# VectorE's order of work in the MLP chunks of a two-layer decoder trunk: two modulation rows instead of three ahead of an up block, and low parts and evacuations of the down half reordered

## The reference, cut to what matters

```python
u = modulate(h, sh_f, sc_f)                                  # u = h * (1 + sc_f) + sh_f
y = jnp.square(jax.nn.relu(u @ mlp_w_up[layer])) @ mlp_w_down[layer]
h = layer_norm(DEEPNORM_ALPHA * h + (1 + g_f) * y, ...)      # up: 1024 -> 4096, down: 4096 -> 1024
mod = (silu(c) @ ada_w[layer] + ada_b[layer])                # six vectors of 1024; two more for K/V
```

## Time and profile before

| | |
|---|---|
| time, median of 3 runs | 2198.84 us (2197.66 to 2198.94) |
| profiled execution | 2198.61 us, span of its trace 2196.9 us |
| TensorE | 2144.9 us busy, 98% of the span, 9984 matmuls |
| VectorE | 1419.3 us, 65% |
| ScalarE | 820.0 us, 37% |
| GpSimd | 373.6 us, 17% |
| granted TensorE clock | 0.997 of full speed on average |

### The profile page before, as it was taken

How to read it: one execution, slowest core, us unless ns; L and a number is a source line. 1 busy time by engine, 2 the same in 40 slices (tenths; PEclk the granted TensorE clock), 3 DMA queues, 4 the chain that set the end, 5 groups by cost and what they waited for, 6 DMA issues and landing times.

```text
span 2196.9 us, 28310 instructions
## 1 busy us (share of the span) xinstructions
PE 2144.9 (98%) x9984; PEld 1730.2 (79%) x9984; DVE 1419.3 (65%) x2223; ACT 820.0 (37%) x1457; POOL 373.6 (17%) x273
## 2 busy tenths in 40 slices
PE   6999999999999999999999999999999999999998
PEld 5888888878887787788887876677888888888886
DVE  7423656578576676776768566767747547557556
ACT  4201445161224234233347456546222422422432
POOL 0000220010033032130200022321003303303304
PEclk9999999999999999999999999999999999999999
DMA  7434653314413423314122110211211021021021
GB/s 291 142 98 133 117 131 101 105 39 134 130 63 95 125 66 115 113 59 134 48 96 85 43 39 20 78 58 33 64 58 58 21 74 57 20 75 57 19 77 77
DMA packets 52433, 183.96 MB, mean 84 GB/s; under 512 B 7472, under 2 KB 7648, under 8 KB 52352
## 3 DMA queue, kind: packets, MB, share of 16 engines
q1 hardware_dynamic: 44640, 161.50, 22.8%
q0 software_dynamic: 4944, 16.96, 3.6%
q10 hardware_dynamic: 2768, 4.41, 0.5%
HBM read 174.43 MB, written 8.42 MB: 83 GB/s over the span
## 4 chain that ended last, share of the span: by engine, by line
issue 44%; PE 41%; POOL 8%; DVE 3%; ACT 2%; DMA 1%; SPq 1%; POOLq 0%; ACTq 0%; DVEq 0%
PE ps L2054 11%; PE ps L2056 11%; PE ps L2055 11%; POOL whi L678 4%; POOL wlo L678 2%; PE ps L2519 1%; POOL h_blocks L673 1%; PE ps L2549 1%; PE ps L2533 1%; DMA resid<-in_xt 1%; PE ps L2157 1%; PE ps L2298 1%; PE ps L2283 1%; PE ps L2287 1%; DVE stats L1572 0%
## 5 line engine op out<-in xcount | busy, mean ns | idle before, releaser
L2054 PE MATMUL ps<-uhi,whi 128*128 128x512 f32 x1152 | 451.6, 392 | 11.3 <-DVE wlo L1700 5.0
L2055 PE MATMUL ps<-ulo,whi 128*128 128x512 f32 x1152 | 448.4, 389 | 0.0
L2056 PE MATMUL ps<-uhi,wlo 128*128 128x512 f32 x1152 | 448.3, 389 | 0.0
L2054 PE MATMUL ps<-whi,uhi 128*128 128x512 f32 x704 | 288.2, 409 | 2.4 <-ACT resid L1111 2.2
L2056 PE MATMUL ps<-whi,ulo 128*128 128x512 f32 x704 | 276.1, 392 | 0.0
L2055 PE MATMUL ps<-wlo,uhi 128*128 128x512 f32 x704 | 275.4, 391 | 0.0
L2054 PEld LDWEIGHTS ps<-uhi,whi 128*128 128x128 f32 x1152 | 216.2, 188 | 65.2 <-issue 7.3
L1740 DVE TENSOR_TENSOR resid<-ps,resid 128x512 f32<-128x512 f32 x336 | 217.9, 680 | 54.8 <-PE ps L2056 53.7
L2056 PEld LDWEIGHTS ps<-uhi,wlo 128*128 128x128 f32 x1152 | 216.3, 188 | 45.3
L2055 PEld LDWEIGHTS ps<-ulo,whi 128*128 128x128 f32 x1152 | 216.3, 188 | 44.0
L1021 ACT ACTIVATE h_blocks<-ps 128x512 f32<-128x512 f32 x96 | 57.2, 596 | 516.5 <-PE ps L2056 516.5
(11 more groups left out here) (300 smaller groups left out, 3542.1 us busy)
## 6 DMA issues: line engine op xcount, KB each, us to landing
stage<-in_stream SPq DMA_DIRECT2D x276, 512.0 KB, 3.6
aux<-in_early SPq DMA_DIRECT2D x8, 512.0 KB, 7.1
early_place<-in_early SPq DMA_DIRECT2D x8, 512.0 KB, 14.2
resid<-in_xt SPq DMA_DIRECT2D x8, 512.0 KB, 15.9
resid<-in_x POOLq DMA_DIRECT2D x8, 512.0 KB, 9.5
resid_dram<-resid ACTq DMA_DIRECT2D x8, 512.0 KB, 2.6
resid<-resid_dram POOLq DMA_DIRECT2D x8, 512.0 KB, 3.6
out<-resid SPq DMA_DIRECT2D x7, 512.0 KB, 2.6
```

The costliest lines, as they stand in the source:

```text
L2054: pe.matmul(dst, left_hi, right_hi, start=start, stop=False, skip_group_check=more)
L2055: pe.matmul(dst, left_hi, right_lo, start=False, stop=False, skip_group_check=more)
L2056: return pe.matmul(dst, left_lo, right_hi, start=False, stop=stop, skip_group_check=more)
```

## The change

In the seven-product chunks of layer 0 the load stream and VectorE take two modulation rows ahead of `up_low(2)` and not three; one stays between `up_low(2)` and `up_low(3)`, and five and not four follow later. In the down half of all twelve chunks VectorE's order changes in three places: `low_of(4, 1, 6)` goes ahead of the evacuation of P4,0; the evacuations of P1,2 and P1,3 go ahead of `up_low(8)`; and `up_low(9)` goes behind `add("P6", 0)` and `low_of(4, 8, 14)`. No instruction is added or taken away.

```diff
     for c in range(CHUNKS):
         if c in SEVEN:
             w(*[W_MLP0 + 8 * c + j for j in SEVEN_LOADS[:4]])
-            ada(SC_KV + c, range(3))
+            ada(SC_KV + c, range(2))
             w(W_MLP0 + 8 * c + 2)
-            ada(SC_KV + c, range(3, 4))
+            ada(SC_KV + c, range(2, 3))
             w(W_MLP0 + 8 * c + 3)
-            ada(SC_KV + c, range(4, K))
+            ada(SC_KV + c, range(3, K))
             w(*[W_MLP0 + 8 * c + j for j in SEVEN_LOADS[6:]])
...
                 if with_ada:
-                    for k in range(3):
+                    for k in range(2):
                         vector(k)
                 up_low(2)
                 if with_ada:
-                    vector(3)
+                    vector(2)
                 up_low(3)
...
                 if with_ada:
-                    for k in range(4, K):
+                    for k in range(3, K):
                         vector(k)
...
                 add("P7", 3)
                 v.wait_ge(h_sums, 4 * q0 + 4 + 4 * i)
-                add("P4", 0)
                 low_of(4, 1, 6)
-                add("P4", 1, 2, 3)
+                add("P4", 0, 1, 2, 3)
                 low_of(5, 0, 8)
                 add("P2", 0, 1)
                 low_of(2, 7, 10)
                 add("P2", 2, 3)
                 add("P1", 0)
                 low_of(3, 6, 12)
-                add("P1", 1)
+                add("P1", 1, 2, 3)
                 up_low(8)
-                add("P1", 2, 3)
-                up_low(9)
                 add("P6", 0)
                 low_of(4, 8, 14)
+                up_low(9)
                 add("P6", 1, 2, 3)
```

## The result

The changed kernel takes 2210.55 us (median, 2209.73 to 2212.76, 6 runs) against 2198.93 us (2197.66 to 2200.70, 6 runs) of the kernel before: ratio 1.0053, 95% interval 1.004 to 1.0066. It is slower, by 11.6 us; 14 were forecast (2213, range 2200 to 2217). The span of the profiled execution grew from 2196.9 to 2209.0 us.

The account below looks back on a forecast made before the run. TensorE, busy 98% of the span, was taken as the bound, with pauses left to win. Down half 22.8 + 0.9 less up half 9.5 gave +14.2 us on 2198.61, forecast 2213 us, range 2200 to 2217.

Parts of the forecast that it names:

- Up half: Six chunks of layer 0: two TensorE pauses per chunk on up weights' low parts go; gain 9.5 us.
- w3's load cycle: Up half, layer 0: from w2's low part to w3's high part, taken as 3.7 us; 4.6 would be too late.
- The tail of modulation rows: Layer 0, five rows behind `low_of(4, 5, 3)`: cost nothing, some 1 us of 2.9 left at the second half sum.
- `low_of(4, 1, 6)` ahead of P4,0: Down half, all 12 chunks: low part ends as before, P4,0's evacuation now behind it, P2 starts later: +0.53 us a chunk.
- The second race: Down half: `low_of(5, 0, 8)` asks 0.08 us after GpSimd's third low part and loses; P2,3 pauses: +1.65 us a chunk.
- Rival 1: Down half: VectorE's `low_of(5, 0, 8)` beats GpSimd's third low part, pause at P2,3 gone: 2192 us; chance 0.12.
- P1's evacuations ahead of `up_low(8)`: Down half: P1,2 no longer waits for `up_low(8)`, so the wait ahead of P6,2 goes: -0.28 us a chunk.
- P5,1: Down half, layer 1: `up_low(9)` later delays P6,1's evacuation, whose bank P5,1 wants: 0.15 us per chunk, +0.9 in all.
- The sum: Whole kernel: 22.8 + 0.9 - 9.5 = +14.2 us on 2198.61, so 2212.8; chance of the forecast 0.68.

Follow-up runs that it names:

- experiment 7: The changed kernel with GpSimd's first low part of each chunk waiting for one more high part of ScalarE (eighth, not seventh): 2188.62 us, ratio 0.9946.
- experiment 3: The changed kernel with `low_of(4, 1, 6)` back behind the evacuation of P4,0: 2183.89 us, ratio 0.993 to the kernel before.
- experiment 5: The changed kernel with `low_of(4, 1, 6)` one evacuation further forward, ahead of that of P7,3: 2179.83 us, ratio 0.9909 to the kernel before.
- experiment 4: The changed kernel with `low_of(5, 0, 8)` moved ahead of the evacuation of P4,3: 2192.01 us, ratio 0.9968 to the kernel before.
- experiment 1: The changed kernel with the down half of the kernel before, so only modulation rows and their loads change: 2188.10 us, ratio 0.9949.
- experiment 6: The changed kernel with `low_of(4, 1, 6)` ahead of P7,3's evacuation and `low_of(5, 0, 8)` ahead of P4,3's: 2186.00 us, ratio 0.9936.

## Why the prediction was right

**Up half, -9.5 us.** Measured alone -11.1 (interval about -8 to -14). The two pauses went in all six chunks; the 3.7 us taken for w3's load cycle was 3.8. The low part of w3 ended at 672.48; this chunk lies 0.64 us later than before, so TensorE's turn was at 673.2, and 0.8 us were to spare. The tail of modulation rows cost nothing, as forecast, but not for the reason given. The prediction looked at the second half sum and saw some 1 us left. The last up group's evacuation stands behind the first half sum's high part, and there 0.00 to 0.28 us were left. In the third chunk `low_of(4, 1, 6)` came 0.24 us later for it (0.35 behind GpSimd's start, not 0.11), and its wait at the port hid this. In experiment 7, where that wait is gone, such a lateness cost 0.5 us in one chunk.

**`low_of(4, 1, 6)` ahead of P4,0, +0.53 a chunk.** Measured +0.54. It started 0.60 earlier, lost to GpSimd by 0.11, ended where it had ended, and P4,0's evacuation came on top. Experiment 3 takes the move back, experiments 5 and 7 turn the race round in two ways; each gives what the arithmetic gave to within 3 us.

**The second race, +1.65 a chunk.** Measured 1.50 + 0.11 = 1.61, and 1.59 to 1.63 over all twelve chunks. This was the step with the greatest doubt, 0.08 us between the two starts (0.08 to 0.11 measured), and carried 20 of the 23 us. The size was worked out; that so small a gap goes GpSimd's way rested on two places with another pair of instructions, and the same trace has six places where a gap of 0.08 goes VectorE's way (last section), so a part of this hit is luck. Rival 1 needed VectorE to win here; the earlier trace rows told otherwise and held. Experiment 4 gave 18.5 us back by one evacuation; 12 x 1.61 is 19.3.

**P1's evacuations ahead of `up_low(8)`, -0.28 a chunk, 3.4 us.** Measured 4.2 by experiments 3 and 1, within their spread.

**P5,1, +0.15 a chunk in layer 1.** The smallest term: the trace has 0.06 to 0.10.

**The sum** of 14.2 (23.7 less 9.5) came out as 11.6 by medians and 12.1 by the spans. Measured term by term the down half is 12 x (0.54 + 1.61 - 0.28) + 0.5 = 22.9. The up half was sized about right: taken by starts, the two pauses of the kernel before are 1.41 to 1.87 us a chunk, 9.7 in all. The six chunks of layer 0 follow each other at 83.84 us in experiment 1 and at 85.54 before, 1.70 x 6 = 10.2. That makes 12.7, 0.6 above the spans. In layer 1, where only the down half changed, chunks follow each other at 84.49 us instead of 82.56: 1.93, where the terms give 0.54 + 1.61 - 0.28 + 0.08 = 1.95.

The Trainium skill's rule on the shared port (SBUF — State Buffer, "Who interferes with whom"), that issue order decides who blocks, is borne out by experiment 7, in which only the time at which GpSimd asks was changed and 21.9 us went.

## What to carry to other kernels

Where VectorE and GpSimd both run instructions whose two inputs lie in SBUF, as the low parts here, an instruction moved forward is worth nothing until it passes the other engine's claim, and an instruction placed behind it then bears the whole wait: look for durations far above an instruction's shortest one, find the other engine's instruction that ends just before it (here 1.1 us before a held low part of VectorE ends, 2.3 before one of GpSimd), and compare their starts. A pause on an evacuation can have its cause one low part earlier. Moving a low part past one evacuation (0.6 us) gave 1.5 us a chunk in experiment 4, 2.2 in experiment 3 and 2.6 in experiment 5, and took 0.5 in experiment 6, so order such lists by who asks first. Leave some room between claims: in experiment 7 a lead of 0.83 us shrank to 0.29 in one chunk.

## What the runs showed of the hardware

The order on the port held to small gaps: VectorE starting 0.11, 0.08 and 0.06 us behind GpSimd waited for its whole instruction (3.39, 3.40 and 3.42 us instead of 1.21), also where GpSimd's instruction followed directly on another of its own, at whose end the port might have been taken. I had not expected it to be so regular: in the changed kernel the first gap is 0.11 or 0.12 us in eleven chunks and 0.35 in one, the second 0.08 to 0.11 in all twelve, and VectorE waited each time. A wait added to GpSimd made the kernel 21.9 us faster.

The pair of the earlier trace rows, in the mixer, shows the same with both signs, since it falls a little differently in each of the nine traces. Where VectorE started 0.03 to 0.34 us behind GpSimd it was held, in each case until 0.55 us after GpSimd's end. Where it started 0.02 to 0.31 us ahead, it took its 0.68 or 0.69 us and GpSimd was held, for 0.88 to 1.16 us instead of 0.64. The smallest lead is in experiment 1, GpSimd and then VectorE:

```profile
286.18 1.16 POOL L626 TENSOR_SCALAR_AFFINE_SELECT dmat<-dmat 128x512 f32<-128x512 f32 x1 [1.67 <-ACT dmat L828]
```

```profile
286.16 0.68 DVE L1421 TENSOR_TENSOR qk<-decay_rows,qk 128x512 f32<-128x512 f32 x1
```

The listed start does not decide for every pair. In layer norm GpSimd has an instruction of one column (L657, 0.26 us alone). Six times in the trace of the kernel before VectorE starts 0.08 us behind it and is not held (0.68 us each), while GpSimd takes 0.81 to 1.41, GpSimd and then VectorE:

```profile
460.42 1.41 POOL L657 TENSOR_SCALAR nmr<-moments,rstd 128x1 f32<-128x1 f32 x1
```

```profile
460.50 1.28 DVE L1547 TENSOR_TENSOR ulo<-u_whole,uhi 128x512 fp32r<-128x512 f32 x2
```

Why this pair differs is open. For a gap this small, take the winner from rows of the same pair of instructions.
